# Which small load goes first: the input, c and the identity at the start of a hybrid encoder block

## The reference

```python
c_act = jax.nn.silu(c)
mods = jnp.split(c_act @ w_ada[l] + b_ada[l], 9, axis=-1)
sh1, sc1, g1, sh2, sc2, g2, sh3, sc3, g3 = mods
h = modulate(rmsnorm(x, norm_g[l, 0]), sh1, sc1)
x = x + 0.5 * g1[:, None, :] * swiglu(h, w_ffn1_in[l], w_ffn1_out[l])
h = modulate(rmsnorm(x, norm_g[l, 1]), sh2, sc2)
# ... h @ w_mix_in feeds a bidirectional HGRN2 group and a windowed attention group ...
x = x + g2[:, None, :] * mixed
h = modulate(rmsnorm(x, norm_g[l, 2]), sh3, sc3)
x = x + 0.5 * g3[:, None, :] * swiglu(h, w_ffn2_in[l], w_ffn2_out[l])
```

## Time and profile before

| | |
|---|---|
| device time, median of 3 | 1026.16 us |
| profiled execution | 1026.21 us |
| its span | 1024.4 us |
| PE busy | 1017.1 us, 99% |
| DVE busy | 803.8 us, 78% |
| ACT busy | 505.3 us, 49% |
| c is turned on PE at | 3.15 us |
| first half of x used at | 6.70 us |
| second half of x used at | 9.47 us |
| first feed-forward product at | 15.72 us |

### The profile page before, as it was taken

One profiled execution on the slowest core, in us unless ns is written; L12 is line 12 of the kernel. 1 busy time (PEld: TensorE's weight loads), 2 busy tenths in 40 slices (PEclk: granted clock), 3 DMA queues, 4 the chain that ended last, 5 costly groups with the idle time before them and its releaser, 6 DMA issues.

```text
span 1024.4 us, 16787 instructions
## 1 busy us (share of the span) xinstructions
PE 1017.1 (99%) x6276; PEld 902.6 (88%) x6276; DVE 803.8 (78%) x1179; ACT 505.3 (49%) x778; POOL 44.5 (4%) x32
## 2 busy tenths in 40 slices
PE   9999999999999999999999999999999999999998
PEld 7888999999888888888888898888999999988886
DVE  5989889988987889878888549778988888745524
ACT  6637555555322254782635773454655555522221
POOL 0000000000000140000200000420000000000000
PEclk9999999999999999999999999999999999999999
DMA  9654343434777443822121031222233332363313
GB/s 346 238 165 150 118 143 103 147 121 174 287 269 249 134 164 94 276 83 83 42 72 32 2 83 42 83 82 83 90 116 97 107 112 93 124 246 123 123 41 83
DMA packets 101218, 133.59 MB, mean 130 GB/s; under 512 B 19217, under 2 KB 84621, under 8 KB 101046
## 3 DMA queue, kind: packets, MB, share of 16 engines
q1 hardware_dynamic: 100702, 130.76, 38.6%
q10 hardware_dynamic: 472, 2.24, 0.6%
HBM read 130.88 MB, written 4.21 MB: 132 GB/s over the span
## 4 chain that ended last, share of the span: by engine, by line
PE 91%; DVE 6%; ACT 1%; DMA 1%; issue 1%; SPq 0%; DVEq 0%; ACTq 0%
PE bank L2056 15%; PE bank L2057 14%; PE bank L2058 14%; PE bank L2332 11%; PE bank L2331 11%; PE bank L2330 11%; PE bank L2434 2%; PE bank L2535 2%; PE bank L2628 1%; DVE w_lo L1265 1%; PE bank L2521 1%; PE bank L2218 1%; PE bank L2204 1%; PE bank L2210 1%; DVE tmod L1349 1%; PE bank L2510 1%
## 5 line engine op out<-in xcount | busy, mean ns | idle before, releaser
L767 ACT ACTIVATE w_hi<-w_raw 128x2048 fp32r<-128x2048 f32 x47 | 89.9, 1914 | 203.0 <-PE bank L2058 191.4
L1265 DVE TENSOR_TENSOR w_lo<-w_raw,w_hi 128x2048 fp32r<-128x2048 f32 x47 | 109.5, 2331 | 94.0 <-ACT w_hi L767 94.0
L2330 PE MATMUL bank<-t_hi,left_hi 128*128 128x256 f32 x544 | 154.0, 283 | 0.0
L2331 PE MATMUL bank<-t_lo,left_hi 128*128 128x256 f32 x544 | 154.0, 283 | 0.0
L2332 PE MATMUL bank<-t_hi,left_lo 128*128 128x256 f32 x544 | 153.9, 283 | 0.0
L2056 PE MATMUL bank<-a_hi,w_hi 128*128 128x512 f32 x352 | 137.4, 390 | 0.3 <-DVE w_lo L1265 0.3
L2058 PE MATMUL bank<-a_hi,w_lo 128*128 128x512 f32 x352 | 137.0, 389 | 0.0
L2057 PE MATMUL bank<-a_lo,w_hi 128*128 128x512 f32 x352 | 137.0, 389 | 0.0
L2056 PE MATMUL bank<-h_hi,w_hi 128*128 128x512 f32 x336 | 133.3, 397 | 0.2 <-DVE w_lo L1265 0.2
L2058 PE MATMUL bank<-h_hi,w_lo 128*128 128x512 f32 x336 | 130.9, 390 | 0.0
L2057 PE MATMUL bank<-h_lo,w_hi 128*128 128x512 f32 x336 | 130.8, 389 | 0.0
(11 more groups left out here) (319 smaller groups left out, 1906.3 us busy)
## 6 DMA issues: line engine op xcount, KB each, us to landing
w_raw<-in_w_ffn_in SPq DMA_DIRECT2D x42, 1024.0 KB, 4.9
ada<-in_w_ada SPq DMA_DIRECT2D x24, 1024.0 KB, 5.0
w_raw<-in_w_ffn_out SPq DMA_DIRECT2D x22, 1024.0 KB, 4.9
w_raw<-in_w_mix_in SPq DMA_DIRECT2D x11, 1024.0 KB, 5.1
shift_in<-in_w_ada SPq DMA_DIRECT2D x4, 1024.0 KB, 8.8
ada_row<-in_w_ada SPq DMA_DIRECT2D x8, 512.0 KB, 4.3
x_nat<-in_x SPq DMA_DIRECT2D x2, 1024.0 KB, 6.1
scale_half<-in_w_ada SPq DMA_DIRECT2D x2, 1024.0 KB, 9.0
```

What stands on the lines that cost most here:

```text
L767: sc.activation(w_hi[n % 2][:], src[:], ACT.Copy).then_inc(whi_done, 1)
L1265: ve.tensor_tensor(w_lo[n % 2][:], src[:], as_f32(w_hi[n % 2][:]), ALU.subtract).then_inc(wlo_done, 1)
L2330: te.matmul(into, wh, xh[:, k, :], start=(opens and k == 0), stop=False, skip_group_check=True)
L2331: te.matmul(into, wh, xl[:, k, :], start=False, stop=False, skip_group_check=True)
```

## The change

The load of c moves from SP's queue to ACT's. ACT also loads a new small tile, `ident_c8`, the 8x8 corner of the identity; both count on `consts_loaded`, and the transposition of c uses `ident_c8`. The load of the whole identity moves from ACT's queue to SP's, right behind the first half of x, and counts on `x_loaded[0]`. Whoever waits for the first half of x now waits for 32 on that semaphore, which means the half and the identity.

```diff
+    ident_c8 = at("ident_c8", [DT, DT], f32, region + 83 * KB)
...
+        X_LOADS = (32, 16)
...
-            sp.dma_start(c_row[:], c.rearrange("o (t q) -> (o t) q", q=P)).then_inc(consts_loaded, 16)
             load_x(0)
+            sp.dma_start(ident[:], ident_c.ap()).then_inc(x_loaded[0], 16)
             sp.dma_start(sink_r[:], attn_sink).then_inc(bias_consts, 16)
...
-            a.dma_start(ident[:], ident_c.ap()).then_inc(consts_loaded, 16)
+            a.dma_start(c_row[:], c.rearrange("o (t q) -> (o t) q", q=P)).then_inc(consts_loaded, 16)
+            a.dma_start(ident_c8[:], ident_c.ap()[0:DT, 0:DT]).then_inc(consts_loaded, 16)
...
             def square(t):
-                a.wait_ge(x_loaded[t // 2], 16)
+                a.wait_ge(x_loaded[t // 2], X_LOADS[t // 2])
...
             def square(t):
-                v.wait_ge(x_loaded[t // 2], 16)
+                v.wait_ge(x_loaded[t // 2], X_LOADS[t // 2])
...
             pe.wait_ge(consts_loaded, 32)
-            te.transpose(bank[2][:, 0:DT], c_row[:], ident[0:DT, 0:DT]).then_inc(c_step, 1)
+            te.transpose(bank[2][:, 0:DT], c_row[:], ident_c8[:]).then_inc(c_step, 1)
...
             spin(4)
-            pe.wait_ge(x_loaded[0], 16)
+            pe.wait_ge(x_loaded[0], X_LOADS[0])
             turn(bank[1], x_nat, 0, (0, 1))
```

## The result

The changed kernel takes 1028.96 us, the median of 12 runs, against 1026.47 us for 12 runs of the kernel before beside them; the ratio is 1.0032, with a 95% interval of 1.0023 to 1.0041. It is slower, by 2.5 us between the medians and 0.32% by the ratio. Its twelve runs fall into two groups, nine from 1028.25 to 1029.18 us and three from 1032.76 to 1032.97 us. The forecast of 1026.0 us and its range up to 1028.0 us both missed; the time is nearest to the rival named last, to which I gave 0.07.

What follows compares the result with a forecast made beforehand. PE bounds the kernel, busy 1017.1 of 1024.4 us. x's second half comes 0.24 us earlier, but late c leaves PE ready at 9.37 against 9.49 us: 1026.21 - 0.12 = 1026.1, as a median 1026.0 us; range 1025.7 to 1028.0 us.

Steps and rivals of the forecast that it cites:

- the rival named last: PE's start: c turned at 5.5 us, spins at the low clock, +2.2 us, 1028.4 us; chance 0.07.
- The place of the loss: Ahead of the products: time moves only by as much as PE's first useful work moves.
- The sign that I had named for it: First scale sum on PE, 10.20 us before: its shift should be the whole difference.
- The head start of x: DMA stream: x issued 0.47 us earlier, less 0.23 us for the identity; second half 0.24 us earlier.
- The landing of c: Corner load on ACT's queue: c turned at 4.8 us, 1.65 us later than before.
- my upper bound: Latest turn of c on PE: 1.3 + 3.4 + 0.8 = 5.5 us.
- b_ada's wait: Load on q10 behind x's first half: 2.7 us from issue to first packet, used for the corner.
- The clock: PE's spins behind c: 2.4 GHz again from close to 4.8 us, eight records in 1.7 us.
- the clock rises later: PE idle before c, spins take 3.4 us, second half 1.5 us later: 1027.7 us; chance 0.28.
- ACT: Square of tile 0 up to 0.5 us later, still ending before x's second half lands.
- c lands promptly: Small loads through before x's stream; all of the 0.24 us gain stays: 1025.9 us; chance 0.18.

Runs made afterwards that it cites:

- the swapped order: Kernel before with the first half of x issued ahead of c on SP, identity still on ACT's queue; 1028.9 us, ratio 1.0040.
- the second experiment: Changed kernel with c back as SP's first load, leaving only the identity's move and the corner on ACT; 1026.46 us, ratio 0.9999.
- the eight-spin version: Changed kernel with eight spins instead of two ahead of the turn of c and none behind it; 1026.05 us, ratio 0.9995.
- The low clock with an early c: Kernel before without the four spins behind the turn of c, no load moved; 1028.65 us, ratio 1.0023.
- x first, c second, spins ahead: Kernel before with x's first half ahead of c on SP, seven spins ahead of c's turn, none behind; 1026.19 us, ratio 0.9997.

## Why the prediction was wrong

**The place of the loss: right.** The claim that the time moves only by what PE's first useful work moves held to 0.1 us in the profiles of the changed kernel: the first product is later by 6.70 us and the span longer by 6.7 us in the first, by 2.07 and 2.1 us in the last. The sign that I had named for it, the time of the first scale sum, fails: that moved by 5.21 us (10.20 to 15.41 us) and by 2.45 us (10.20 to 12.65 us). The scale sums do not take the same time in all profiles, so the measure has to stand behind them.

**The head start of x: more for the first half, none shown for the second.** The first half was used 0.61 us earlier, at 6.09 us, where I had 0.24 us. But the second half, at which I also put a gain of 0.24 us, is used between 9.22 and 9.65 us in the seven profiles that have the changed order of loads, at 9.45 us on average, against 9.47 us before. These profiles scatter by 0.4 us, and no gain stands out of that.

**The landing of c: the first step that failed.** "I take 1.3 + 2.7 + 0.8 = 4.8 us, by the nearest row": it was 6.24 us, past even my upper bound of 5.5 us. I had taken b_ada's wait as a fixed wait behind x. Issued 0.27 us behind x, b_ada had seven of x's packets per engine ahead of it; the corner, issued 0.78 us behind, had nearly all sixteen, and 64 KB of identity issued in between. The later a load is issued behind x, the more of x seems to be lined up ahead of it: 0.02 us behind, the corner passed between 2.4 and 2.8 us; at 0.14 us, `c_row` and, in the swapped order, the identity passed beside x's packets; at 0.78 us the corner had none before 5.0 us. That is a pattern over a few issues, not a rule tested by itself, and b_ada's place does not always fit it: issued 0.36 us behind x in the second experiment, its queue had no packet from 2.4 to 5.0 us; issued 0.45 us behind x where the sinks' and the table's loads stand ahead of x, ten packets passed on its queue between 4 and 5 us. Nor was the corner tried at 0.78 us without the identity ahead of it. I had written that its place was worse than b_ada's, and then used b_ada's number. The corner's issue, too, came at 1.52 us and not at 1.3 us, because `c_row`'s took 0.60 us on ACT's queue.

**The clock: the step that decides the time.** The forecast rested on "if it rises about then again". It did not: PE stood idle for 3.03 us, the spins behind c ran at 0.43 us each, and in the slower group the low clock lasted into the scale sums, to about 19 us. Kept busy with spins, PE has the high clock behind a c that is as late, and 1026.89 us; idle with an early c, 1028.65 us. Of the 2.07 us of the faster group, 0.69 us is thus c's lateness at the high clock, with four spins still behind c, and the other 1.4 us the clock; in the slower group the clock's part is 6.0 us. These parts are differences of single profiles. The rival "the clock rises later" had the mechanism and the price of one case, 1.5 us with c at 4.8 us. With c at 6.2 us its own sum gives 6.4 + 3.4 + 2.62 = 12.4 us for the second half's turn, 2.9 us later than 9.49 us; measured in the faster group are 12.11 us there and 2.07 us at the first product, since the scale sums then no longer wait for their weights. I gave it 0.28 and its extension 0.07, on the ground that half of the earlier stretch stays busy. The Trainium skill, "TensorE: Matmul & The Clock Gate", section "What's actually happening", says that the throttled state is the default and that activity releases it; the two kernels that differ in spins alone agree (3.78 us against 1.99 us for the same eight records).

**ACT: right that it costs nothing, wrong by how much it moves.** `cact` and the table load moved by 2.5 us, and the square of tile 0 began at 8.14 us, 1.4 us later than before and not 0.5 us at most. It ended at 9.28 us, still ahead of the second half of x.

**The rival "c lands promptly": wrong.** The 0.6 us to the first byte that it took from the Trainium skill, "DMA: Bandwidth & Descriptors", section Specifications, was not what the corner got behind x: it had no packet for 3.5 us from its issue. Issued 0.33 us ahead of x, in the second experiment, its sixteen packets had all passed by 2.4 us, at most 1.5 us from its issue.

What stays open is why the clock came up near 10 us in some runs and after the scale sums began in others, with PE busy without a gap from 6.2 us in both, and what the slower runs with four spins ahead look like. The kernel before, too, had one run at 1030.22 us among the 17 beside the eight-spin version, and two near 1028.4 us among the 32 beside the four experiments from "The low clock with an early c" to "x first, c second, spins ahead". Their granted clock is 0.997 and 0.998, where all other runs of that kernel have 0.999 or 1.000; that would fit a stretch at the low clock, but no trace of such a run was taken, and the slower group of the changed kernel shows 0.999.

## What to carry to other kernels

Issue a small load that TensorE's first instructions need before the first large load; another queue does not by itself save it. Here two that were issued 0.02 and 0.14 us behind the megabyte came through early, and one 0.78 us behind waited for nearly all of it. When a change makes TensorE wait before its real work, price the wait and the clock behind it apart, and look for filler work that stands on the wrong side of the wait: seven filler steps ahead of the wait and none behind, instead of two and four, took the loss away (1028.96 us to 1026.04 us). And where a bound is read from a neighbouring load's wait, ask what of it scales with the distance.

## What the runs showed of the hardware that I had not expected

The column of the granted clock is no witness for the first microseconds: in the first profile it shows 1.00 in every stretch that I read, also in this one, in which eight spin records took 3.78 us at half pace (length, busy times, clock, DMA share, GB/s):

```profile
6.20:10.00 3.80, 3.76 (x9) 2.93 (x10) 1.47 (x3) 3.06 (x6) 0.00 (x0) 1.00 0.98 353
```

The durations tell: 1.87 us or 1.02 us for the table's product. The clock can also stay at the lower level far longer than one would plan for: in the first profile PE was busy without a gap from 6.24 us, and the 32 scale records from 15.41 us still took 5.62 us, against 3.74 us for the same records in the profile with the earlier rise. Even unbroken spins don't fix the moment: with seven and eight of them ahead of c, c was turned at 6.28 us in one profile and at 7.02 and 7.47 us in others, because the slow spins lasted longer.
